# A fused two-block transformer kernel: a buffer at the seam of the expert layer, a new order of selection units and row requests, and gate projections moved among the attention items

## What is computed

```
s = einsum('tpcd,pckd->tpck', q, sub_keys)          # 8 heads x 2 x 128 keys
top, pos = top_k(top_k(s1, 16) + top_k(s2, 16), 16); g = softmax(top)
y = einsum('tpk,tpkd->td', g * gelu(einsum('tpkd,td->tpk', u[idx], t)), v[idx])

# second block
w   = exp(log_sigmoid(z) + suffix sum of log_sigmoid(-z))     # stick-breaking
y_a = (w @ v * silu(sb_z)) @ w_branch_a
y_b = (softmax(causal scores) @ v * silu(mla_z)) @ w_branch_b
x   = x + gate * ((sigmoid(g_a) * y_a + sigmoid(g_b) * y_b) @ w_out)
```

## Time and profile before

| | us |
|---|---|
| median of 3 runs | 2378.25 |
| lowest, highest | 2375.66, 2378.37 |
| the profiled execution, its own time | 2373.85 |
| its span, first to last instruction | 2372.1 |

### The profile page before, as it was taken

The page is one execution under the profiler, slowest core; times in us unless marked ns, Lnnn a source line. Parts: engine busy times, 40 slices in busy tenths (PEclk is TensorE's granted clock), DMA queues, the critical chain, the costliest instruction groups (busy, mean ns, idle before and its releaser), DMA issues. The chain is left out here.

```text
span 2372.1 us, 31727 instructions
## 1 busy us (share of the span) xinstructions
PE 2209.9 (93%) x12601; PEld 1968.8 (83%) x12601; DVE 1696.4 (72%) x2801; ACT 919.4 (39%) x1203; POOL 620.9 (26%) x354
## 2 busy tenths in 40 slices
PE   5999888989999998999999899999999897899997
PEld 2888676766899998999999899999999674576775
DVE  6555667773579999889876787788786656756543
ACT  4222234333233333566653233333333533576323
POOL 0000042321347776333334433333331000000000
PEclk8999999999999999999999999999999898899999
DMA  7567400011237777999999999999996222111222
GB/s 258 204 226 237 170 32 1 1 72 65 90 108 237 245 245 237 331 355 340 359 345 388 350 352 353 352 361 350 351 355 219 81 89 71 54 54 63 81 89 71
DMA packets 178100, 488.69 MB, mean 206 GB/s; under 512 B 13696, under 2 KB 80384, under 8 KB 166432
## 3 DMA queue, kind: packets, MB, share of 16 engines
q1 hardware_dynamic: 141088, 352.43, 43.4%
q0 software_dynamic: 36864, 134.23, 14.7%
HBM read 432.08 MB, written 52.43 MB: 204 GB/s over the span
## 5 line engine op out<-in xcount | busy, mean ns | idle before, releaser
L1077 PE MATMUL ps<-h_high,u_high 128*128 128x384 f32 (+1 forms) x1216 | 429.1, 353 | 19.0 <-POOL u_low L1295 10.9
L1078 PE MATMUL ps<-h_low,u_high 128*128 128x384 f32 (+1 forms) x1216 | 421.2, 346 | 0.0
L1079 PE MATMUL ps<-h_high,u_low 128*128 128x384 f32 (+1 forms) x1216 | 421.0, 346 | 0.0
L1077 PE MATMUL ps<-w_high,v_high 128*128 128x384 f32 x1024 | 344.8, 337 | 11.3 <-DVE w_low L1712 11.3
L1079 PE MATMUL ps<-w_high,v_low 128*128 128x384 f32 x1024 | 343.8, 336 | 0.0
L1078 PE MATMUL ps<-w_low,v_high 128*128 128x384 f32 x1024 | 343.8, 336 | 0.0
L1077 PEld LDWEIGHTS ps<-h_high,u_high 128*128 128x128 f32 x1216 | 230.9, 190 | 34.0 <-POOL u_low L1295 13.0
L1445 ACT ACTIVATE v_high<-v_raw 128x2048 fp32r<-128x2048 f32 x64 | 122.6, 1916 | 346.7 <-PE ps L1079 346.7
L1077 PE MATMUL ps<-h_high,w_high 128*128 128x512 f32 x560 | 226.8, 405 | 19.7 <-DVE w_low L346 5.6
L1079 PEld LDWEIGHTS ps<-h_high,u_low 128*128 128x128 f32 x1216 | 231.1, 190 | 8.0
L1078 PEld LDWEIGHTS ps<-h_low,u_high 128*128 128x128 f32 x1216 | 231.4, 190 | 7.0
(11 more groups left out here) (434 smaller groups left out, 4208.0 us busy)
## 6 DMA issues: line engine op xcount, KB each, us to landing
v_raw<-in_peer_v SPq DMA_DIRECT2D x64, 1024.0 KB, 6.3
w_raw<-in_w SPq DMA_DIRECT2D x99, 512.0 KB, 3.5
u_first<-in_uT SPq DMA_DIRECT2D x32, 1024.0 KB, 5.9
u_second<-in_uT SPq DMA_DIRECT2D x32, 1024.0 KB, 6.4
xT<-in_late_w SPq DMA_DIRECT2D x56, 512.0 KB, 4.4
gelu_up<-gelu SPq DMA_DIRECT2D x128, 192.0 KB, 7.0
gates<-gates_sb SPq DMA_DIRECT2D x12, 2048.0 KB, 12.3
weighted<-gelu_up SPq DMA_DIRECT2D x64, 384.0 KB, 6.5
```

Of the source, the lines that this page charges most:

```text
L1077: pe.matmul(out, wh, mh, start=start, stop=False)
L1078: pe.matmul(out, wh, ml, start=False, stop=False)
L1079: return pe.matmul(out, wl, mh, start=False, stop=stop)
```

## The change

In the expert layer: units 0 to 15 go at groups 6, 7, 8, 9, 10, 12, 13, 15, 17, 19, 21, 24, 26, 28, 30, 32 in the order of `UNIT_ORDER`; the turn and the spreading start three groups earlier; row requests come one group later in POOL's program and the last ones one group earlier in the plan. At the seam, slab 0 has a buffer of its own, the loads come earlier in SP's program, and groups 0 and 1 are weighed and split ahead of the row work. In the second block, two heads of `uqm` share a piece, tiles go to slots by their cost, and `ga` 0, 1 and `sz` 0, 1, 2 move in front of slot 16 (88 split products on each side); PE's scores and DVE's masks wait for one item, not for two, and DVE masks an item of the next slot behind each finished item.

```diff
-TURN_AT = 40
-SPREAD_AT = 41
-SPREAD_G = 28
-EARLY, MIDDLE = 40, 66
+TURN_AT = 37
+SPREAD_AT = 38
+SPREAD_G = 31
+EARLY, MIDDLE = 36, 70
+UNIT_ORDER = [(0, 0), (0, 1), (1, 0), (1, 1), (2, 0), (3, 0), (2, 1), (3, 1)] + [(c, t) for t in (2, 3) for c in range(4)]
...
-    return OUT_G + 2 + 2 * u if u < 4 else OUT_G + 10 + 2 * (u - 4)
+    return OUT_G + (2, 3, 4, 5, 6, 8)[u] if u < 6 else OUT_G + 9 + 11 * (u - 6) // 5
...
-    return GROUPS - 7 + 7 * (n - EARLY - MIDDLE) // (PICKS - EARLY - MIDDLE)
+    return GROUPS - 8 + 7 * (n - EARLY - MIDDLE) // (PICKS - EARLY - MIDDLE)
...
-    return n * (U_G - 3) // PICKS
+    return 1 + n * (U_G - 4) // PICKS
...
+        first_gates = sb("gates_in", [P, BLOCKS * 2 * GE * TB])
...
-              for x in u_raw]
+              for x in (first_gates, u_raw[0])]
...
+            gate_pair(0)
+            load(0)
             spill(GROUPS - 4)
-            load(0)
+            load(1)
+            spill(GROUPS - 3)
+            spill(GROUPS - 2)
             sp.wait_ge(u_split, OUT_PIECES + WQ_G + U_G - 1)
-            gate_pair(0)
-            spill(GROUPS - 3)
-            load(1)
-            spill(GROUPS - 2)
-            sp.wait_ge(u_split, OUT_PIECES + WQ_G + U_G)
             gate_pair(1)
             spill(GROUPS - 1)
...
-                for n in picks_at[x + OUT_G]:
+                for n in picks_at[x + OUT_G - 1]:
...
+            high_v(1)
+            high_w(1)
             act.wait_ge(row_used, PICKS)
...
-            weigh(0)
-            low_v(0)
-            low_w(0)
+            for g in range(2):
+                weigh(g)
+                low_v(g)
+                low_w(g)
...
-    for h in range(NH):
-        piece("uq", h, [("uqm", h)])
+    for i in range(4):
+        piece("uq", i, [("uqm", 2 * i), ("uqm", 2 * i + 1)])
+    piece("kn", 0, [("kn", j) for j in range(4)])
+    piece("ga", 0, [("ga", 0)])
+    piece("sz", 0, [("sz", 0)])
+    piece("kn", 1, [("kn", 4 + j) for j in range(4)])
+    piece("ga", 1, [("ga", 1)])
     piece("kv", 0, [("kv", t) for t in range(4)])
+    for i in (1, 2):
+        piece("sz", i, [("sz", i)])
+    halfway = len(tiles)
+    for i in (2, 3):
         piece("ga", i, [("ga", i)])
+    piece("sz", 3, [("sz", 3)])
+    for i in range(4):
+        piece("ga", 4 + i, [("ga", 4 + i)])
         piece("bra", i, [("bra", 2 * i), ("bra", 2 * i + 1)])
...
+        for first, end, slot, count in ((PROJECTED, HALFWAY, 0, HALF), (HALFWAY, ATTENDED, HALF, slots - HALF)):
+            sizes = [PRODUCTS2[TILES2[j][0]] for j in range(first, end)]
+            for x, j in enumerate(range(first, end)):
+                fill[slot + sum(sizes[:x]) * count // sum(sizes)].append(j)
...
-                if p:
-                    pe.wait_ge(acted, 2 * p)
...
+                    if p:
+                        pe.wait_ge(acted, 2 * p - 1 + s)
...
-                dve.wait_ge(scored, 2 * (n // 2) + 2)
+                dve.wait_ge(scored, n + 1)
...
+            mask(0)
+            mask(1)
             for p in range(slots):
-                if p < PAIRS:
-                    mask(2 * p)
-                    mask(2 * p + 1)
                 for j in fill[p]:
                     if j in FIRST2:
                         low(TILES2[j][2] + 1)
                     evac(j)
+                for n in (2 * p, 2 * p + 1):
+                    if n < N:
+                        finish(n)
+                    if n + 2 < N:
+                        mask(n + 2)
                 if p >= 2 and (p - 2) % TT == TT - 1:
                     store((p - 2) // TT)
-                if p < PAIRS:
-                    finish(2 * p)
-                    finish(2 * p + 1)
```

More of the change, by code:

```diff
@@ L1201, in unit_of @@
         def unit_of(u):
[L1203 removed]
+            c, t = UNIT_ORDER[u]
+            return c, order[t]
         def batches_at(g, j):
@@ L1218, in spill, with gate_pair, load @@
                     sp.dma_start(gelu[g - OUT_G - WQ_G][:, j, :], gel[:, x % 4, :]).then_inc(spilled[x % 4], 16)
+            def gate_pair(i):
+                sp.dma_start(gr[i % 2].rearrange("p n j t -> p n (j t)"), gates[i]).then_inc(g_in[i % 2], 16)
+            def load(g):
+                if g >= 2:
+                    sp.wait_ge(v_split, g - 1)
+                sp.dma_start(v_raw[:, g % 2], v[g]).then_inc(v_in[g % 2], 16)
+                if g >= 2:
+                    sp.wait_ge(w_split, g - 1)
+                sp.dma_start(w[:, g % 2], gelu[g]).then_inc(w_in[g % 2], 16)
             written = 0
@@ L1289, in _ @@
             pool.tensor_tensor(u_low[:, 1], u_raw[1][:], u_high[:, 1].bitcast(F32), ALU.subtract).then_inc(u_split, 1)
-            for x in range(WQ_G + U_G):
+            for x in range(WQ_G + U_G + 1):
                 if x + OUT_G < SPREAD_AT:
@@ L2026, in tile @@
                         pe.wait_ge(t_low, G0 + 5)
-                    w3, src = weights(j, 0, 3), [(ghi[:, t, :], glo[:, t, :]) for t in range(3)]
+                    w3, src = weights(j, 3 * (n % 2), 3), [(ghi[:, t, :], glo[:, t, :]) for t in range(3)]
                 elif kind == "kn":
```

53 lines of the change are left out of this document (19 added, 34 removed).

## The result

The kernel after takes 2384.18 us (median of 20 runs, 2379.19 to 2393.72) against 2375.66 for the kernel before on the same chip: a ratio of 1.0038, 95% interval 1.0031 to 1.0044. It is 8.5 us slower; 36 us of gain were forecast. The profiled execution took 2385.11, its span is 2383.3, 11.2 more than before.

A forecast was written before the change was run, and what follows sets the result against it. PE, busy 2209.9 of 2372.1 us, was taken as the bound, except three short stretches bound by DVE's program. Gains of 12 + 14 + 10 = 36 us off 2378.25 gave 2342 us, range 2316 to 2366.

The forecast's parts named there:

- Part A: Selections and row requests, group 12 to the turn: 12 us of gain, bounds 20 and minus 8.
- That is even, and about 2 us are lacking over nine units.: Selections from group 13 on: 19.2 us of PE per unit against 19.4 of DVE.
- I take 1.2 us more for each of six selections, 7 us.: Selections: allowance for DVE and POOL blocking each other once POOL's start is untied from DVE's dot.
- the three bounds that were to prove the forecast wrong: Stick stretch over 134 or under 110, turn wait over 15 us, group 2 over 25 us behind the up-projection.
- buys another 8.4 us: Turn moved from four to five groups behind the last unit: 8.4 us for shift, six dots and softmax.
- the spreading costs 0: Spreading over 31 groups for 28, same 48 batches: no cost, as PE has no stall there to lose.
- Part B: Seam between up- and down-projection: 14 us of gain from 15.9 lost, bounds 16 and 2.
- The row work behind it has no one waiting but itself: Seam: DVE weighs group 1 ahead of dots and rows, so delayed row work holds up nothing else.
- Some us of cover: Seam: group 72's spills, behind 3 MB more, free Gelu tiles PE needs only at group 0.
- Part C: Gates among the stick items: stick stretch +15, softmax stretch -25, 10 us of gain, bounds 28 and minus 13.
- Rival 2: Selections: the block of DVE and POOL eats Part A, giving 0; time 2354, chance 0.12.
- rival 5: Stick slots: gate products wholly on top of DVE's chain at low clock, Part C minus 35; 2387, chance 0.06.

The follow-up runs named there:

- e2: Kernel before with the selection part (Part A) alone: unit order and steps, turn, spreading, row requests; 2397.57 us, ratio 1.0092.
- e7: e5 with the row requests one step later, old unit order, turn and spreading; 2378.80 us, ratio 1.0014.
- e11: Kernel after with ACT's exponential of the own tile at group 16 instead of 14; 2379.48 us, ratio 1.0013.
- e9: e6 with 70 key rows in the spreading instead of 66, the last 18 at three a group, no dots left after the up-projection; 2365.77 us.
- e10: e9 with 28 key rows before the turn instead of 40, and 82 in the spreading instead of 70; 2398.45 us, ratio 1.0088.
- e16: e6 with the turn at group 39 and spreading from group 40 over 29 groups; 2381.37 us, ratio 1.0022.
- e3: Kernel before with the seam part (Part B) alone; 2378.52 us, ratio 1.0010.
- e14: e6 with the value rows' terms spread from group 2 on instead of group 1; 2360.22 us, ratio 0.9934.
- e4: Kernel before with the attention part (Part C) alone: moved gate and sz projections, new order of masks and finishes; 2369.15 us, ratio 0.9967.
- e8: e7 with the new unit order and steps too, turn at group 40 and spreading over 28 groups as before; 2386.71 us, ratio 1.0037.
- e5: Kernel before with Part B and Part C, value rows spread from group 1 on instead of group 0; 2368.36 us, ratio 0.9968.
- e6: e5 with the spill of group 73 ahead of the loads of group 1 instead of behind them; 2365.09 us, ratio 0.9958.

## Why the prediction was wrong

**Part A, forecast 12 us of gain, took 21 (e2).** Four steps of it failed.

- "That is even, and about 2 us are lacking over nine units." The balance took a selection as 15.3 us, its length where it begins in step with POOL. Units that follow without a gap meet the low part elsewhere: 18.4 to 22.1 for six of the first eight, most of them ahead of the nine that I had balanced. The filled idle time of 24.2 us brought 8.0. The period of the nine is 20.5 us, where my sign said 19.3.
- "I take 1.2 us more for each of six selections, 7 us." The block was the right mechanism, and for the nine selections even the size was near: they take 7.9 us more. What had no term is the rest, 8.3 us in the first seven units and what the later request does elsewhere. Its first victim in e7 was the row numbers, 4.22 us at one step of a queue with no slack, and e7 prices the later request alone at 10.4 us, where I had let it buy time. The sign I gave for it, the small step's median above 1.31, was a bad one: it is 1.29, because other steps are hit instead. The sign that did speak was PE's waits for POOL's low part, 19.5 us where I had said under 4; the three bounds that were to prove the forecast wrong all held (128.9, 4.57 and 22.0 us).
- ACT's exponential of the own tile had no term at all. I moved the own tile's last unit behind two foreign ones and did not ask who waits for the shift: 12.5 us of ACT, 7.5 of PE. By e11 this was 5 to 6 us.
- The turn "buys another 8.4 us": group 37 instead of 40 is 26 us less of PE's time, but the last selection came 10.8 us earlier, 13.9 with the later start of this execution. I had counted the distance in groups and not the end of the selections in us. The wait at the turn itself was small (4.57), as I had said; the price lies in the groups around it, 11.5, 11.2, 14.9, 13.9 and 11.9 us for 34 to 38.

That the spreading costs 0 isn't borne out: groups 41 to 68 take 281.8 us against 283.6, but with 43 batches instead of 48, and e9, e10 and e16 show them not to be indifferent to rows or layout. From the turn to the last up product after takes 394.1 us against 356.3, of which three groups more are 25.2. Groups 69 to 74 take 5.2 us more (56.3 against 51.1), which I had not looked at.

**Part B, forecast 14, measured nothing alone (e3).** The 10.5 us in the trace of after are not its own: 8.9 are there in e2, without it. What it adds on top of A and C was not run. The loads came early, as I said. "The row work behind it has no one waiting but itself" failed: the row terms of groups 0 and 1 stand ahead of group 2's weighting. "Some us of cover" for the spills of group 72 failed: there was none, ACT stood 13.3 us. With the first mended and group 73's spill ahead of group 1's loads (e14 against e4) the part gives 8.8. ACT still stands 12.9 us for group 72, and 5.2 to 5.7 us of wait are left ahead of group 0. My limit for group 2's start, 25 us behind the last up product, was kept by after (22.0) thanks to lines I had costed under A (e2 alone has 23.6).

**Part C, forecast 10, measured 7 to 8.** Right in sum and sign in both stretches (+20.1 and -28.6 in e4, forecast +15 and -25), wrong inside. The order of masks, 7 in my sum, is worth 9.1; the moved projections, with three terms of 21.5 against 25, are worth nothing. I saw 28 us of idle PE and priced the gate products at 2 us each, with PE "so far under cover"; they cost their full time.

Rival 2 (the block eats part A) named the mechanism and stopped at A = 0, and my lower bound of minus 8 was too narrow by 13 us. The stick stretch stayed far under the 160 us of rival 5, whose time of 2387 came near the measured one by luck, for another reason.

Beside this, e7 and e8 share out part A on the base of e5: later request +10.4, order and steps +7.9, turn with spreading and last requests -2.9, of which the turn and the spreading are a loss in their stretch and the last requests a gain at the seam. The other order of adding them was not tried. Single causes inside these prices (the block, the late exponential, the turn) are read from traces; only the exponential was undone by itself (e11).

## What to carry to other kernels

When an engine is busy over 97% of a stretch, ask of each edit what it does to that engine's queue in microseconds; filling its idle time brings only what contention leaves, and here that was a third. A wait can be what keeps two engines apart (so e7 suggests): before it is removed, look at what the freed engine will run and which steps of the other it will meet. And before work is moved into a stretch because an engine idles there, change the order alone first: here the order was the whole gain, and the moved products went in at full price.

## What was unexpected of the hardware

A wait of 5.3 us on GpSimd seems worth more than it cost: the kernel without it is 10.4 us slower (e7, which moves all row requests and not this one alone). The block depends on the kind of step: MAX8 steps ran at 0.87 us beside a low part of 4.62, while a TENSOR_TENSOR that starts 0.05 us behind one took 5.12 for 0.68. And four rows of 0.5 MB more in 28 groups cost 3.9 us (e9), sixteen about 27 against e6 (e10: 312.3 against 284.9), with DMA's share not above 0.93; why is open.
